# The last layer's attention scores in three rounded products, with the keys kept once

## The chip, the cores and the metric

The kernel runs on one core of a Trainium2 chip. The metric is the device time of one execution in microseconds; the span given with a profile is the time from its first to its last instruction.

## What is computed

A block of two attention layers over 512 tokens of width 1024 is followed by one hybrid layer. Its first half is an attention with three branches: over compressed keys, over chosen blocks of keys, and over a window. With 512 tokens, eight blocks of 64 and the best eight chosen, and with a window of 512, the last two branches each come to plain causal attention, with keys and values of their own. There are eight query heads of 64 elements; four of them share a key head (g).

```python
s_cmp = jnp.einsum('bgrsd,bgcd->bgrsc', qh, k_cmp) * SCALE
p_cmp = masked_softmax(s_cmp, cmp_end[None, :] <= pos[:, None])
...
_, sel_idx = lax.top_k(imp, top_n)

q_rot = partial_rope(qh, pos)
ks_blk = partial_rope(kvh(ks), pos).reshape(B, NSA_KV, n_sel, SEL_BLOCK, HEAD_DIM)
...
s_win = jnp.einsum('bgrqd,bgkd->bgrqk', qc, kwc) * SCALE
p_win = masked_softmax(s_win, w_mask)
o_win = jnp.einsum('bgrqk,bgkd->bgrqd', p_win, vwc.astype(f32))
...
o = g[..., 0:1] * o_cmp + g[..., 1:2] * unblock(o_sel) + g[..., 2:3] * unblock(o_win)
```

## The kernel before

**Rounded parts.** All large products of the kernel are made of three: each f32 operand is split into a high part (a copy in the rounded type, F32R) and a low part (the f32 value minus the high part, rounded too), and high x high, high x low and low x high are added in one PSUM bank. `second` holds, for some stretches of an SBUF tensor, a twin of type F32R at the same addresses; `rounded(v)` gives the twin of a view, `read_back(v)` reads it as f32. For the weights ScalarE writes the high part (`high`, line 1310) and GpSimd the low part in four quarters (`lower`, line 2506). The small products of the attention, the scores of the last layer among them, are plain f32 products.

**Banks and order.** Each engine has a list of its own instructions in the order of the program. TensorE takes the eight PSUM banks in turn: `begin(key, consumer)` makes TensorE wait until the bank of the key eight before is evacuated, and notes whether ScalarE ("a") or VectorE ("v") empties it; `end` tells that it is filled. `take` on the consumer waits for the filled bank, `give` tells that it is drained, `evacuated` waits for that. All matmuls have line 468 (`mm`), ScalarE's copies line 1281 (`copy`), semaphore waits of their own line 316 or 303.

**Before the steps.** Queries and keys of the last layer lie with tokens on partitions: q2 (for the compressed branch), q2r (rotated), kd (rotated keys of both branches b, each head twice side by side). After the product "hid" TensorE transposes them, for each of the four token tiles i: keys ("qp", i) (line 818), ("qr", i) (818) and ("kz", i) (822). ScalarE empties these banks (after a wait for three memsets of GpSimd, C_clear): qp into qTp and qr into qTr, both scaled by 1/8, and kz in two copies, partitions 0 to 63 into kz[..., e = 0, ...] and 64 to 127 into kz[..., e = 1, ...]; the other halves hold the zeros of a memset of 4096 columns on GpSimd (line 2617). Ahead of i = 2 ScalarE rounds the weights Cog0 (`high(HI[("Cog", 0)])`), behind the last tile Cog1. TensorE goes on with `gate_c(0)`, 24 products with Cog0, for whose quarters it waits on GpSimd, with kcmp and vcmp, `gate_c(1)`, the compressed scores `scores_c`, `gate_c(2)` and so on. VectorE makes hid_t (2148), then waits for the gate (2122), kcmp and vcmp.

**The steps.** The attention of the two branches runs in NSTEP = 12 steps s; each has four units u = 4s + m, one bank each. `cell(s, m)` gives head pair j = s // 3, query tile i, branches and e = m % 2 (head 2j + e, whose 64 elements lie on partitions 64e to 64e + 63). With k = s % 3: for k = 0 the units are query tiles 0, 0, 1, 1 with both branches in a bank (256 and 512 columns), for k = 1 query tile 2 (384 columns) for each branch and e, for k = 2 tile 3 (512 columns). TensorE's order is scoresN(s), transN(s-1), pvN(s-2): the scores and then the four causal masks (bf16, line 468, from identb and causalb), the transposes of the probabilities (line 904), and the products with the values. So the keys of a step are four ("NS", u), four ("NT", u), one ("NO", s). VectorE takes the maxima (2221) of step s, then, when ScalarE's exponentials are done, the reciprocals (2228) and the scaling of the probabilities (2236), ahead of it the output of step s-3 (`outN`, 2208, into mixA). ScalarE's order is the four units' exponentials of step s (1634), then the four copies of transposes of step s-1 (1281); in step 7 and step 9 it rounds weights for the next stage behind them.

**Areas.** The arena is one SBUF tensor. fl (the input of "hid") and mixA both lie at 15552 to 17600; kz takes 8192 to 12288.

Of the kernel before, what the change touches and what calls it, by code (L numbers as in the profile page):

```python
# [106 lines left out]
def program(nc, A, out):  # L107
    ctx = ExitStack()
    with ctx:
# [29 lines left out]
        arena = sb2("arena", [P, NARENA], (0, 12288), (19456, 6144))  # L139
# [230 lines left out]
        kz = area(8192, 4096).rearrange("p (b g e t) -> p b g e t", b=2, g=2, e=2)  # L370
# [74 lines left out]
        def _(pe):  # L445
# [368 lines left out]
            for i in range(NT):  # L814
                for name, src in (("qp", q2), ("qr", q2r)):
                    b = begin((name, i), "a")
                    for j in range(4):
                        ins = nc.tensor.transpose(b[:, j * P:(j + 1) * P], src[:, i, j * P:(j + 1) * P], ident)
                    end(ins)
                b = begin(("kz", i), "a")  # L820
# [45 lines left out]
            gate_c(1)  # L866
            evacuated(pe, ("kz", NT - 1))
# [12 lines left out]

            def scoresN(s):

                bs = []
                for m in range(4):
                    j, i, brs, e = cell(s, m)
                    n, nb, es = (i + 1) * P, len(brs), slice(64 * e, 64 * e + 64)
                    b = begin(("NS", 4 * s + m), "a")
                    k = ap(kz[es, brs[0], j // 2, e, :], [(2048, nb), (1, n)])
                    mm(b[:, 0:nb * n].rearrange("p (b n) -> p b n", b=nb), qTr[es, j, i * P:(i + 1) * P], k, True, False)
                    bs.append(b)  # L890
# [378 lines left out]
        def _(act):  # L1269
# [309 lines left out]
            act.wait_ge(S("C_clear"), 3)  # L1579
            for i in range(NT):  # L1580
                if i == 2:
                    high(HI[("Cog", 0)])
                for name, dst in (("qp", qTp), ("qr", qTr)):
                    key = (name, i)
                    b = take(act, key)
                    give(copy(dst[:, :, i * P:(i + 1) * P], b[:, :].rearrange("p (j t) -> p j t", j=4), 0.125), key)
                key = ("kz", i)
                b = take(act, key)
                for e in range(2):
                    es = slice(64 * e, 64 * e + 64)  # L1590
                    ins = copy(ap(kz[es, 0, 0, e, :], [(1024, 4), (1, P)], i * P), b[es, :].rearrange("p (j t) -> p j t", j=4))
                give(ins, key)
# [157 lines left out]
        def _(dve):  # L1750
# [397 lines left out]
            give(STT(hid_t, thh, 1.0, b[:, 0:256], ALU.add, ALU.mult), "hid")  # L2148
# [546 lines left out]
```

## Time and profile before

| | us |
|---|---|
| median of 3 runs | 1234.92 |
| lowest and highest | 1231.48, 1236.01 |
| profiled execution, its own time | 1235.75 |
| its span | 1234.0 |
| TensorE matmul busy | 1146.0 (93%) |
| TensorE weight load busy | 963.2 (78%) |
| VectorE busy | 592.1 (48%) |
| ScalarE busy | 509.0 (41%) |
| GpSimd busy | 452.0 (37%) |
| mean granted TensorE clock, share of full | 0.979 |

PE is the TensorE matmul, PEld its weight load, which overlaps it, DVE is VectorE, ACT ScalarE, POOL GpSimd, SP the queue of the loads. A row of the time line gives a start, a duration, the engine, line and operation, what is written and read, the rows and columns of the array (64*128), partitions and columns of the operand, the count of instructions merged, and in brackets the idle time before and what ended it. A matmul's duration holds its way through the array, so the pace of a stream is read from the starts of its instructions. An f32 type in these rows may be a rounded operand; such operands have "parts" in their names.

### The profile page before, as it was taken

The page shows a single profiled execution, that of the slowest core. Times are in us where ns is not written, and L with a number is a line of the kernel's source. Part 1 is how long each engine was busy: PE and PEld are TensorE (multiplying, and loading weights), DVE is VectorE, ACT ScalarE, POOL GpSimd, SP SyncE. Part 2 cuts the span into 40 slices and gives each one's busy share as a digit, 9 for nine tenths or more (in the row PEclk, how much of TensorE's full clock was granted, in tenths as well). Part 3 has the DMA queues.
Part 4 walks back from the last instruction along what each step waited for, and adds up shares of the span by engine and source line. Part 5 has one row for each costly group of instructions (what it writes and reads, how often), then busy time and mean ns, then how long its engine had stood idle before and what let it go on. Part 6 is the DMA issues. An engine that isn't in the chain of part 4 may idle for free.

```text
span 1234.0 us, 24860 instructions
## 1 busy us (share of the span) xinstructions
PE 1146.0 (93%) x10339; PEld 963.2 (78%) x10339; DVE 592.1 (48%) x1376; ACT 509.0 (41%) x1038; POOL 452.0 (37%) x391
## 2 busy tenths in 40 slices
PE   3999999999898999899998959988999999999995
PEld 3988887889898998656798958966777787778862
DVE  5000003842728158788417275026872577335546
ACT  4232224852424432688523264242883421233321
POOL 5744484884445445301344326320006452000000
PEclk9999999999999999999999989999999899999998
DMA  7433243323121232100231231262002223100001
GB/s 211 142 104 102 76 129 106 83 55 103 43 95 40 98 103 89 49 1 1 70 103 35 80 126 52 69 188 69 2 2 69 69 72 111 55 24 3 4 2 68
DMA packets 73178, 89.60 MB, mean 73 GB/s; under 512 B 1993, under 2 KB 66634, under 8 KB 72938
## 3 DMA queue, kind: packets, MB, share of 16 engines
q1 hardware_dynamic: 70136, 78.65, 20.0%
q0 software_dynamic: 2416, 8.26, 2.7%
q8 instruction: 82, 1.34, 0.5%
q10 hardware_dynamic: 514, 1.11, 0.4%
q14 instruction: 30, 0.25, 0.1%
HBM read 83.75 MB, written 4.26 MB: 71 GB/s over the span
## 4 chain that ended last, share of the span: by engine, by line
PE 79%; DVE 9%; ACT 5%; POOL 3%; issue 3%; DMA 1%; ACTq 1%; DVEq 0%; POOLq 0%
PE bank L468 73%; PE bank L736 2%; POOL ring_parts L2506 2%; ACT arena L1281 1%; PE bank L646 1%; DVE stat L1782 1%; PE bank L904 1%; DVE arena L1805 1%; ACT ring_parts L1310 1%; DVE stat L1783 1%; DVE x L1802 1%; ACT arena L1634 1%; ACT arena L1397 1%; DMA vrow<-in_cmp_pos_v 1%; DVE arena L1793 1%
## 5 line engine op out<-in xcount | busy, mean ns | idle before, releaser
L2506 POOL TENSOR_TENSOR ring_parts<-ring,ring_parts 128x512 fp32r<-128x512 f32 (+1 forms) x236 | 306.8, 1333 | 372.7 <-ACT ring_parts L1310 284.1
L468 PE MATMUL bank<-ring_parts,hT_parts 128*128 128x256 f32 x1664 | 331.0, 285 | 12.6 <-POOL arena_parts L2512 7.8
L468 PE MATMUL bank<-hT_parts,ring_parts 128*128 128x512 f32 x896 | 285.3, 397 | 8.7 <-DVE x L1802 4.8
L468 PEld LDWEIGHTS bank<-ring_parts,hT_parts 128*128 128x128 f32 x1664 | 269.8, 192 | 15.3 <-issue 11.2
L1281 ACT ACTIVATE arena<-bank 128x512 f32<-128x512 f32 (+3 forms) x356 | 166.7, 528 | 261.7 <-PE bank L468 253.7
L468 PE MATMUL bank<-ring_parts,arena_parts 128*128 128x256 f32 x1088 | 257.7, 285 | 3.4 <-POOL hT_parts L2523 3.4
L468 PE MATMUL bank<-arena 64*64 64x64 f32 (+6 forms) x3440 | 217.2, 275 | 7.6 <-ACT arena L1634 2.9
L468 PEld LDWEIGHTS bank<-hT_parts,ring_parts 128*128 128x128 f32 x896 | 171.0, 191 | 49.5 <-issue 6.6
L468 PEld LDWEIGHTS bank<-arena 64*64 64x64 f32 (+2 forms) x3440 | 157.1, 141 | 61.3 <-issue 23.5
L468 PEld LDWEIGHTS bank<-ring_parts,arena_parts 128*128 128x128 f32 x1088 | 190.8, 192 | 4.3 <-POOL hT_parts L2523 3.8
L1310 ACT ACTIVATE ring_parts<-ring 128x2048 fp32r<-128x2048 f32 (+1 forms) x59 | 111.3, 1886 | 76.9 <-PE bank L468 76.9
L468 PE MATMUL bank<-arena_parts,ring_parts 128*128 128x512 f32 x256 | 101.2, 395 | 0.0
L1857 DVE SCALAR_TENSOR_TENSOR arena<-arena,bank 128x512 f32<-128x512 f32 x8 | 5.5, 687 | 172.0 <-ACT arena L1385 172.0
L468 PE MATMUL bank<-x_parts,ring_parts 128*128 128x512 f32 x192 | 77.2, 402 | 0.0
L468 PEld LDWEIGHTS bank<-arena_parts,ring_parts 128*128 128x128 f32 x256 | 48.0, 188 | 10.7
L2523 POOL TENSOR_TENSOR hT_parts<-hT,arena_parts 128x512 fp32r<-128x512 f32 x16 | 20.4, 1280 | 92.1 <-ACT arena_parts L1336 91.9
L2512 POOL TENSOR_TENSOR arena_parts<-arena,hT_parts 128x512 fp32r<-128x512 f32 x26 | 34.4, 1350 | 44.2 <-ACT hT_parts L1315 44.2
L468 PE MATMUL bank<-ring,arena 64*64 64x64 f32 (+3 forms) x512 | 49.2, 304 | 0.8 <-DMA ring<-in_cmp_w_v 0.8
L1511 ACT ACTIVATE arena<-bank,stat 128x512 f32<-128x512 f32 x64 | 43.2, 688 | 14.1 <-PE bank L468 6.7
L1924 DVE TENSOR_TENSOR x<-x,bank 128x256 f32<-128x256 f32 x32 | 13.4, 420 | 70.9 <-PE bank L468 70.9
L2043 DVE TENSOR_REDUCE stat<-bank 128x1 f32<-128x512 f32 x64 | 39.8, 684 | 14.3 <-PE bank L468 14.3
L1946 DVE SCALAR_TENSOR_TENSOR arena<-arena,bank 128x256 f32<-128x256 f32 x32 | 13.4, 419 | 64.2 <-PE bank L468 58.5
(240 smaller groups left out, 1440.5 us busy)
## 6 DMA issues: line engine op xcount, KB each, us to landing
ring<-in_a_w_in SPq DMA_DIRECT2D x16, 1024.0 KB, 5.4
ring<-in_w_in SPq DMA_DIRECT2D x15, 1024.0 KB, 5.5
ring<-in_b_w_in SPq DMA_DIRECT2D x10, 1024.0 KB, 5.3
ring<-in_ple_w_gate SPq DMA_DIRECT2D x8, 1024.0 KB, 5.1
arena<-rpb_rows POOLq DMA_DIRECT2D x16, 256.0 KB, 3.5
ring<-in_a_w_out SPq DMA_DIRECT2D x4, 1024.0 KB, 5.1
ring<-in_b_w_out SPq DMA_DIRECT2D x4, 1024.0 KB, 5.3
ring<-in_w_out SPq DMA_DIRECT2D x4, 1024.0 KB, 5.0
```

Of the source, the lines that this page charges most:

```text
L468: return nc.tensor.matmul(o, l, r, start=start, stop=stop)
L646: ins = nc.tensor.transpose(b[:, o:o + P], pA[:, u % 8, o:o + P], ident)
L736: ins = nc.tensor.transpose(b[:, k * P:(k + 1) * P], pB[u % 8][:, k * P:(k + 1) * P], ident)
L1281: return nc.scalar.activation(o, i, ACT.Copy, scale=scale)
L1310: nc.scalar.activation(rounded(high_slot(n)[:, 0:m]), raw_slot(n)[:, 0:m], ACT.Copy).then_inc(s_whi, 1)
L1511: give(nc.scalar.activation(pB[u % 8], b[:, :], ACT.Exp, bias=stat[:, c:c + 1], accum_out=stat[:, c + 8:c + 9]), key)
L1924: give(TT(xs, xs, b[:, 0:w], ALU.add), key)
L1946: give(STT(tp[:, u % 2, :], thp[:, u % 4, :], 1.0, b[:, 0:256], ALU.add, ALU.mult), key)
L2043: nc.vector.tensor_reduce(stat[:, 128 + u % 8:129 + u % 8], b[:, :], X, ALU.max, negate=True)\
L2506: nc.gpsimd.tensor_tensor(rounded(r), r, read_back(high_slot(n)[:, o:o + m // 4]), ALU.subtract)\
L2512: nc.gpsimd.tensor_tensor(rounded(v), v, read_back(tile_of(hTf, tag, i, hf)), ALU.subtract)\
L2523: nc.gpsimd.tensor_tensor(rounded(hT[:, j, :]), hT[:, j, :], read_back(o_high[:, T * j:T * j + T]), ALU.subtract)\
```

## The change

Queries qTr and keys kz of the scores get a high part, written by ScalarE in the rounded type, and a low part, written by VectorE from the same bank and the high part; the low part of the queries lies in mixA, that of the keys in kz_lo, the second half of the old kz. The banks of qr and kz are thus emptied by VectorE, after ScalarE has read them (a new semaphore C_high). The keys lose the axis e: both heads' halves are written by one copy of 128 partitions, the memset is gone, and so is ScalarE's wait for C_clear; VectorE waits for two of these instead of three. TensorE also waits for the last qp. The scores of a unit become three products of 64 rows in place of one plain f32 product; all four banks of a step are taken first, then, for units 0 and 1 and again for 2 and 3, each of the three products is issued for both units in turn. The masks follow as before.

```diff
--- before.py
+++ after.py
@@ -136,7 +136,7 @@
         w2 = sb("w2", [P, 2, 2, HD])
         wa = sb("wa", [P, 512])
         NARENA = 27968
-        arena = sb2("arena", [P, NARENA], (0, 12288), (19456, 6144))
+        arena = sb2("arena", [P, NARENA], (0, 12288), (15552, 2048), (19456, 6144))
         bank = [ctx.enter_context(nc.psum_tensor(f"bank{b}", [P, 512], F32)) for b in range(NBANK)]
         x_kept = nc.dram_tensor("x_kept", [NT, P, D], F32, kind="Internal").ap()
         scratch = nc.dram_tensor("rpb_rows", [16, 1024], F32, kind="Internal").ap()
@@ -367,7 +367,8 @@
         q2r = area(2048, 2048).rearrange("p (i n) -> p i n", i=NT)
         qTp = area(4096, 2048).rearrange("p (j t) -> p j t", j=4)
         qTr = area(6144, 2048).rearrange("p (j t) -> p j t", j=4)
-        kz = area(8192, 4096).rearrange("p (b g e t) -> p b g e t", b=2, g=2, e=2)
+        kz = area(8192, 2048).rearrange("p (b g t) -> p b g t", b=2, g=2)
+        kz_lo = area(10240, 2048).rearrange("p (b g t) -> p b g t", b=2, g=2)
         vS = area(12288, 1024).rearrange("p (i b n) -> p i b n", i=NT, b=2)
         gt = area(14432, 96).rearrange("p (i n) -> p i n", i=NT)
         pTc = area(14528, 1024).rearrange("p (g t) -> p g t", g=2)
@@ -812,12 +813,12 @@
             used3(("W1V", 1))
             pe.wait_ge(S("C_rope"), 4)
             for i in range(NT):
-                for name, src in (("qp", q2), ("qr", q2r)):
-                    b = begin((name, i), "a")
+                for name, src, consumer in (("qp", q2, "a"), ("qr", q2r, "v")):
+                    b = begin((name, i), consumer)
                     for j in range(4):
                         ins = nc.tensor.transpose(b[:, j * P:(j + 1) * P], src[:, i, j * P:(j + 1) * P], ident)
                     end(ins)
-                b = begin(("kz", i), "a")
+                b = begin(("kz", i), "v")
                 for m in range(4):
                     ins = nc.tensor.transpose(b[:, m * P:(m + 1) * P], kd[:, i, m // 2, (m % 2) * P:(m % 2) * P + P], ident)
                 end(ins)
@@ -864,6 +865,7 @@
                              w2[:, 1, blk, :], blk == 0, blk == 1)
             end(ins)
             gate_c(1)
+            evacuated(pe, ("qp", NT - 1))
             evacuated(pe, ("kz", NT - 1))
             pe.wait_ge(S("C_cmp"), 12)
             scores_c(0)
@@ -878,16 +880,20 @@
             trans_c(3)
 
 
+            qn_parts = [rounded(v[:, :, :]) for v in (qTr, mixA)]
+            kn_parts = [rounded(v[:, :, :, :]) for v in (kz, kz_lo)]
+
             def scoresN(s):
 
-                bs = []
-                for m in range(4):
-                    j, i, brs, e = cell(s, m)
-                    n, nb, es = (i + 1) * P, len(brs), slice(64 * e, 64 * e + 64)
-                    b = begin(("NS", 4 * s + m), "a")
-                    k = ap(kz[es, brs[0], j // 2, e, :], [(2048, nb), (1, n)])
-                    mm(b[:, 0:nb * n].rearrange("p (b n) -> p b n", b=nb), qTr[es, j, i * P:(i + 1) * P], k, True, False)
-                    bs.append(b)
+                bs = [begin(("NS", 4 * s + m), "a") for m in range(4)]
+                for m0 in (0, 2):
+                    for a, c in ((0, 0), (0, 1), (1, 0)):
+                        for m in (m0, m0 + 1):
+                            j, i, brs, e = cell(s, m)
+                            n, nb, es = (i + 1) * P, len(brs), slice(64 * e, 64 * e + 64)
+                            k = ap(kn_parts[c][es, brs[0], j // 2, :], [(1024, nb), (1, n)])
+                            mm(bs[m][:, 0:nb * n].rearrange("p (b n) -> p b n", b=nb),
+                               qn_parts[a][es, j, i * P:(i + 1) * P], k, (a, c) == (0, 0), False)
                 for m, b in enumerate(bs):
                     j, i, brs, e = cell(s, m)
                     nb = len(brs)
@@ -1576,20 +1582,19 @@
             give(copy(gt[:, :, :], b[:, 0:96].rearrange("p (i n) -> p i n", i=NT)), "bgT")
             b = take(act, "hid")
             nc.scalar.activation(thh, b[:, 0:256], ACT.Tanh, scale=0.5).then_inc(S("C_thh"), 1)
-            act.wait_ge(S("C_clear"), 3)
             for i in range(NT):
+                ts = slice(i * P, (i + 1) * P)
                 if i == 2:
                     high(HI[("Cog", 0)])
-                for name, dst in (("qp", qTp), ("qr", qTr)):
-                    key = (name, i)
-                    b = take(act, key)
-                    give(copy(dst[:, :, i * P:(i + 1) * P], b[:, :].rearrange("p (j t) -> p j t", j=4), 0.125), key)
-                key = ("kz", i)
+                key = ("qp", i)
                 b = take(act, key)
-                for e in range(2):
-                    es = slice(64 * e, 64 * e + 64)
-                    ins = copy(ap(kz[es, 0, 0, e, :], [(1024, 4), (1, P)], i * P), b[es, :].rearrange("p (j t) -> p j t", j=4))
-                give(ins, key)
+                give(copy(qTp[:, :, ts], b[:, :].rearrange("p (j t) -> p j t", j=4), 0.125), key)
+                b = take(act, ("qr", i))
+                nc.scalar.activation(rounded(qTr[:, :, ts]), b[:, :].rearrange("p (j t) -> p j t", j=4), ACT.Copy, scale=0.125)\
+                    .then_inc(S("C_high"), 1)
+                b = take(act, ("kz", i))
+                nc.scalar.activation(rounded(kz.rearrange("p b g t -> p (b g) t")[:, :, ts]),
+                                     b[:, :].rearrange("p (j t) -> p j t", j=4), ACT.Copy).then_inc(S("C_high"), 1)
             b = take(act, "hidT")
             for n in range(2):
                 ins = copy(ap(hid[:, n, :], [(64, 2), (1, 64)]), ap(b[:, :], [(P, 2), (1, 64)], 64 * n))
@@ -2146,8 +2151,18 @@
             b = take(dve, "hid")
             dve.wait_ge(S("C_thh"), 1)
             give(STT(hid_t, thh, 1.0, b[:, 0:256], ALU.add, ALU.mult), "hid")
+            for i in range(NT):
+                ts = slice(i * P, (i + 1) * P)
+                for m, (name, low_part, high_part, scale) in enumerate((
+                        ("qr", mixA[:, :, ts], qTr[:, :, ts], 0.125),
+                        ("kz", kz_lo.rearrange("p b g t -> p (b g) t")[:, :, ts],
+                         kz.rearrange("p b g t -> p (b g) t")[:, :, ts], 1.0))):
+                    dve.wait_ge(S("C_high"), 2 * i + m + 1)
+                    b = take(dve, (name, i))
+                    give(STT(rounded(low_part), b[:, :].rearrange("p (j t) -> p j t", j=4), scale, read_back(high_part),
+                             ALU.mult, ALU.subtract), (name, i))
             gatesC([("og", 0)], "C_tanh", Gn)
-            dve.wait_ge(S("C_clear"), 3)
+            dve.wait_ge(S("C_clear"), 2)
 
             b = take(dve, "kcmp")
             for e in range(2):
@@ -2614,7 +2629,6 @@
             nc.gpsimd.memset(kcz[:, :, :, :], 0.0).then_inc(S("C_clear"), 1)
             nc.gpsimd.memset(vcz[:, :, :, :], 0.0).then_inc(S("C_clear"), 1)
             lower(HI[("Cq", 0)])
-            nc.gpsimd.memset(kz[:, :, :, :, :], 0.0).then_inc(S("C_clear"), 1)
             lower(HI[("Cq", 1)], HI[("Cog", 1)])
             pool.wait_ge(S("N_probs"), 4 * NSTEP)
             lower(HI[("R", 6)], HI[("R", 2)])
```

## Rows read from the trace of the kernel before

**Rows 1.** the page's chain that ended last, shares of the span by engine
```profile
PE 79%; DVE 9%; ACT 5%; POOL 3%; issue 3%; DMA 1%; ACTq 1%; DVEq 0%; POOLq 0%
```

**Rows 2.** the chain in order of time before the steps: start us, us, what
```profile
821.48 1.92 ACT ring_parts L1310
823.47 1.27 POOL ring_parts L2506
```

**Rows 3.** TensorE's time line, steps 3 to 6: start us, us, engine, line
```profile
870.69 0.73 PEld L468 LDWEIGHTS bank<-arena 64*128 64x128 f32 x8 [0.17 <-ACT arena L1634]
...
872.18 0.61 PE L468 MATMUL bank<-causalb,identb 128*128 128x256 bf16 x4
...
876.15 1.02 PEld L468 LDWEIGHTS bank<-arena 64*128 64x128 f32 x8 [0.17 <-issue]
...
877.72 0.40 PE L468 MATMUL bank<-causalb,identb 128*128 128x128 bf16 x4
...
881.64 0.30 PEld L468 LDWEIGHTS bank<-arena 64*128 64x128 f32 x4 [0.17 <-ACT arena L1281]
...
883.56 0.40 PE L468 MATMUL bank<-causalb,identb 128*128 128x128 bf16 x4
...
887.42 0.30 PEld L468 LDWEIGHTS bank<-arena 64*128 64x128 f32 x4 [0.17 <-ACT arena L1634]
```

**Rows 4.** groups of instructions in 881.5 to 883.9: busy us, mean ns of one
```profile
L468 PE MATMUL bank<-arena 64*128 64x512 f32 x8 | 2.0, 615 | 0.0
```

**Rows 5.** the time line, weights' products of 256 and 512 columns on TensorE
```profile
795.01 0.40 PE L468 MATMUL bank<-ring_parts,hT_parts 128*128 128x256 f32 x2
...
795.37 0.40 PE L468 MATMUL bank<-ring_parts,hT_parts 128*128 128x256 f32 x2
...
805.05 0.62 PE L468 MATMUL bank<-hT_parts,ring_parts 128*128 128x512 f32 x2
...
805.73 0.62 PE L468 MATMUL bank<-hT_parts,ring_parts 128*128 128x512 f32 x2
```

**Rows 6.** the time line, narrow windows: first copies of transposes, a load
```profile
870.54 0.50 ACT L1281 ACTIVATE arena<-bank 128x384 f32<-128x384 f32 x1
...
876.19 0.63 ACT L1281 ACTIVATE arena<-bank 128x512 f32<-128x512 f32 x1
...
876.88 0.21 PEld L468 LDWEIGHTS bank<-arena 64*128 64x128 f32 x2
...
880.95 0.39 ACT L1281 ACTIVATE arena<-bank 128x256 f32<-128x256 f32 x1
```

**Rows 7.** the time line of step 2: last score's load, masks' matmuls
```profile
865.77 0.29 PEld L468 LDWEIGHTS bank<-arena 64*128 64x128 f32 x2 [0.27 <-ACT arena L1634]
...
866.83 0.40 PE L468 MATMUL bank<-causalb,identb 128*128 128x128 bf16 x4
```

**Rows 8.** TensorE in the time line of step 10, at pvN(8)
```profile
914.26 4.10 PE L468 MATMUL bank<-arena 128*64 128x128 f32 x44 [1.29 <-ACT arena L1634]
```

**Rows 9.** the time line before the steps, on ScalarE, TensorE and VectorE
```profile
817.12 4.34 ACT L1281 ACTIVATE arena<-bank 128x512 f32<-128x512 f32 x8 [0.26 <-PE bank L818]
...
824.88 0.47 PE L468 MATMUL bank<-hT_parts,ring_parts 128*128 128x512 f32 x1 [2.84 <-POOL ring_parts L2506]
...
831.35 0.69 DVE L2122 SCALAR_TENSOR_TENSOR arena<-arena,bank 128x512 f32<-128x512 f32 x1 [13.94 <-ACT arena L1549]
```

**Rows 10.** the time line near 180 us: GpSimd's low parts beside VectorE reading PSUM
```profile
178.95 3.79 POOL L2506 TENSOR_TENSOR ring_parts<-ring,ring_parts 128x512 fp32r<-128x512 f32 x3
...
180.51 0.69 DVE L1857 SCALAR_TENSOR_TENSOR arena<-arena,bank 128x512 f32<-128x512 f32 x1 [4.87 <-ACT arena L1385]
```

**Rows 11.** the time line of GpSimd: the memset of kz and what follows
```profile
764.02 3.51 POOL L2617 MEMSET arena<- 128x4096 f32 x1
769.93 1.30 POOL L2506 TENSOR_TENSOR ring_parts<-ring,ring_parts 128x512 fp32r<-128x512 f32 x1 [2.40 <-ACT ring_parts L1310]
```

**Rows 12.** 845 to 851: busy us (PE, PEld, DVE, ACT, POOL), clock, DMA, GB/s
```profile
845.00:851.00 6.00, 5.25 (x26) 4.58 (x27) 4.44 (x12) 1.19 (x4) 0.00 (x0) 0.74 0.01 3
```

## Prediction

> **What bounds the kernel now.** I read the page's chain first: 79% of it is TensorE [rows 1]. Then I read the same chain in order of time around the last layer's attention, to see which pieces there are not TensorE [rows 2]. Before the attention steps the queue of TensorE stands still for 2.84 us until GpSimd has the first low parts of Cog0 [rows 9]; the chain goes ScalarE rounding (1.92 us), GpSimd (1.27 us), then TensorE [rows 2]. The steps themselves (scoresN, transN, pvN, twelve of them, in groups of three: k = 0, 1, 2) I read in the time line. From the first weight load of the scores of one group (870.69) to that of the next (887.42) is 16.73 us, in which the queue is nearly always busy. The three steps take 5.46, 5.49 and 5.78 us [rows 3]. So TensorE bounds this stage, and a shorter score phase would count in full, if nothing else of TensorE's turn got later.
>
> **The score phases now.** From the first load of the scores to that of the mask they take 1.49, 1.57 and 1.92 us for k = 0, 1, 2 [rows 3]. The last holds four scores of 512 columns in eight records of 615 ns each, but the union is 2.0 us [rows 4]: the scores of e = 0 and e = 1 (partitions 0 to 63 and 64 to 127) run side by side. Two pairs in 1.92 us, less some 0.2 us for the first load and for the change to the mask, is 0.86 us a pair, that is 0.43 us for each of the two records of a plain f32 matmul.
>
> **Three products instead.** No row shows a rounded product of 64 rows. The nearest are the weights' products of 128 rows: three of 512 columns start 0.68 us after the last three (805.05 to 805.73), so 0.227 each; three of 256 columns take 0.36 us, so 0.12 each [rows 5]. In between, 384 columns make 0.173. If a pair costs what one of these costs, the phases become, with the same 0.2 us: 3 x (0.12 + 0.227) + 0.2 = 1.24; 6 x 0.173 + 0.2 = 1.24; 6 x 0.227 + 0.2 = 1.56. That saves 0.25, 0.33 and 0.36 us, 0.94 a group, 3.8 us over four groups. The lower bound of a product is half of a plain record, 0.213 (and 0.107 for 256 columns), as the pairs now have it: then the savings are 0.33, 0.41 and 0.44. The upper bound is that pairs are lost (a rival below). I take the middle one, as it is a measured stream of the same kind of product.
>
> **The four banks taken at once.** This is the step I think decides. Now each score waits for its own bank just before its matmul. After, `begin` runs four times ahead of the first product, so the first product waits also for the fourth bank. In an order of nine keys a step over eight banks, the fourth bank of scoresN(s+1) is that of the first transposes of transN(s-1), and ScalarE copies these only after all exponentials of step s. The waiting TensorE has the whole of scoresN, transN and pvN queued behind it. When are those copies over now? At 870.54 + 0.50 = 871.04, at 876.19 + 0.63 = 876.82, at 880.95 + 0.39 = 881.34, and one group after the first at 871.04 + 16.73 = 887.77; and a load starts 0.06 us later (876.88) [rows 6]. Scores began at 870.69, 876.15 and 887.42 [rows 3]. So in two steps of three the fourth bank comes after the scores have begun. The copies move with the scores of their step, since exponentials wait for maxima and these for the mask. So:
> - k = 0 to 1: 876.88 - 870.69 - 0.25 = 5.94 us, against 5.46: 0.48 longer.
> - k = 1 to 2: here the copy is over at 881.34, before TensorE arrives at 881.64, so TensorE's own work binds: 5.49 - 0.33 = 5.16, 0.33 shorter.
> - k = 2 to 0: 887.83 - 881.64 - 0.36 = 5.83, against 5.78: 0.05 longer.
>
> A group comes to +0.20 us (with the lower bound of a product: +0.40 - 0.41 - 0.03 = -0.04). At the start the steps don't fit this. The scores of step 2 are now issued one by one as ScalarE frees the banks; the last load starts at 865.77 and the mask's matmul at 866.83 [rows 7]. After, all four start at 865.77 - 0.25 = 865.52 and the mask at 867.08, 0.25 later, and the scores of step 3 after the copy: 871.04 + 0.06 + 0.25 = 871.35 against 870.69, +0.66. Steps 3 to 8 add 2 x 0.20. In step 9 ScalarE also rounds weights, and TensorE waits 1.29 us for its next exponentials [rows 8]; that chain follows the scores of step 9, so it stands at +1.06 - 0.25 = +0.81, and the last score phase takes off 0.36. The stage ends +0.45 us later; with the lower bound of a product about -0.3. The 3.8 us are not lost to work, they turn into this wait.
>
> **Copies before the steps.** ScalarE now makes four copies a token tile (qp, qr, two halves of kz): eight in 4.34 us, 0.54 each, then it rounds Cog0 [rows 2, 9]. After, there are three a tile, so the rounding starts two copies earlier: -1.08 us. Its cover is none: TensorE waits 2.84 us for it [rows 9]. What is late next is GpSimd's 1.27 us, which moves along; the later chain over tanh, VectorE and TensorE starts from the same matmuls. VectorE gets eight subtractions of 128x512 out of PSUM, 0.69 us each as the nearest row [rows 10], 5.5 us in all. They follow ScalarE's copies one behind, lie in an idle stretch of VectorE and are over near 826, before anything on that engine is due (its next work starts at 831.35 after 13.94 us of idleness [rows 9]); the banks they free (qr, kz) are wanted one tile or more later. Queued behind them stand the gate product, kcmp and vcmp. Without that cover, each would cost 0.69. Would they slow GpSimd, which then makes the low parts that TensorE waits for? Such an instruction at 180.51 left GpSimd's three tiles at 3.79 us, 1.26 each [rows 10]: no. A rounded output may cost ScalarE nothing or as much as 0.1 us each; the four of them before Cog0's rounding would be 0.4 us.
>
> **At nothing:** the memset of kz leaves GpSimd (3.51 us), but after it GpSimd waited 2.40 us for ScalarE anyway [rows 11]; if that cover were gone it would still be a gain only. No transfer is added or moved; the wait for the clears on ScalarE had long been met; the new waits for qp's last tile and for C_clear 2 as well.
>
> **The sum.** -1.08 + 0.45 = -0.6 us; by the bounds -1.4 to -0.2. The profiled run took 1235.75 us (span 1234.0 us), 0.8 above the median of 1234.92. The runs of before differ by 4.5 us, so I put the sum on the median: 1234.3 us. Half a per cent (6.2 us) is about what a measurement of this kernel can tell from no change.
>
> **Rivals.**
> - The wait for the fourth bank costs nothing (the copies come in time once all is shifted). For it: one step of three has that slack. Against: the two rows above. Then 3.8 + 1.08 come off: 1230.0 us. Chance 0.14.
> - Slower: rounded products of 64 rows don't run side by side. For it: no row has such a product. Against: plain f32 ones do [rows 4]. Each pair then costs double: 1.04 + 1.04 + 1.36 = 3.44 us a group, 13.8 in all, inside the loop of waits: 1248.1 us. It passes the half per cent once half of the pairing is lost. Chance 0.08.
> - Weight loads show in each product (0.1 us, six a step, twelve steps): +7.2, 1241.5 us. Chance 0.04. This is what the page's rule gives.
> - The clock: the granted share was 0.74 in 845 to 851 [rows 12], between its levels of 2.4 and 1.2 GHz; a mean of 0.74 over 6 us is 3.1 us of them at 1.2 GHz, which cost 1.6 us. TensorE has less to do in the steps and waits more, so one such stretch may appear there: 1235.9. Or this one may go: 1232.7. Together 0.10; they lie within the range.
> - The edit doesn't do what it says (rounded copies or products that cost as plain ones): each product of 512 as a plain pair's 0.86 us would show at once as score phases of over 5 us. Chance 0.01.
>
> My forecast has 0.63. The range reaches to the first rival and, upwards, over a lost clock stretch and the scatter of the runs, up to where a quarter of the pairing is lost: 1229.5 to 1239.5 us. Faster by over 0.5% (under 1228.7): 0.06, the first rival with a clock stretch gone. Slower: the three rivals outside the range, 0.08 + 0.04 + 0.01 = 0.13. Within: the rest, 0.81.
>
> **What would show it.** Score phases of 1.24, 1.24 and 1.56 us (steps k = 0, 1, 2) with 12 records each in pairs; the first load of the scores 0.06 us behind ScalarE's first copy in two steps of three, the engine idle 0.3 to 0.6 us before it; the group at 16.9 us; the wait for Cog0's low parts at 1.8 us instead of 2.84. The prediction is wrong if the group falls to 15.8 us (first rival), or if the score phases exceed 2 us (second, third).

## The result and the profile after

| | before | after |
|---|---|---|
| median of 20 runs of each, us | 1235.79 | 1237.96 |
| lowest to highest | 1231.26 to 1237.73 | 1235.06 to 1240.62 |
| profiled execution: its own time | 1235.75 | 1235.06 |
| its span | 1234.0 | 1232.4 |
| mean granted TensorE clock | 0.979 | 0.977 |

The ratio is 1.0018, with a 95% interval of 1.001 to 1.0026: the changed kernel is 2.2 us longer, inside the half per cent, but more than nothing. The sum of the prediction said -0.6. The profiled execution of after is by chance a short one, so the two spans don't show the difference; the stages do. Single executions of 3919.8 us (the kernel before) and 4918.5 us (e11 below) are of the slow kind and are left out of every ratio.

The chain of after covers only part of its span, so I read it for nothing, and read the time line by stages. Its row of shares, beside [rows 1]:

```profile
PE 22%; DVE 1%; issue 1%; ACT 1%; POOL 1%; DVEq 0%; ACTq 0%; POOLq 0%
```

TensorE's time line of steps 3 to 6 in after, beside [rows 3]. Columns as there; in brackets is the idle time before the row and what ended it.

```profile
867.00 0.50 PE L469 MATMUL bank<-arena_parts 64*128 64x256 f32 x4 [0.42 <-ACT arena L1287]
...
868.25 0.61 PE L469 MATMUL bank<-causalb,identb 128*128 128x256 bf16 x4
...
873.04 0.62 PE L469 MATMUL bank<-arena_parts 64*128 64x384 f32 x4 [0.75 <-ACT arena L1287]
...
874.29 0.40 PE L469 MATMUL bank<-causalb,identb 128*128 128x128 bf16 x4
...
878.13 0.72 PE L469 MATMUL bank<-arena_parts 64*128 64x512 f32 x4
...
879.72 0.40 PE L469 MATMUL bank<-causalb,identb 128*128 128x128 bf16 x4
...
884.07 0.50 PE L469 MATMUL bank<-arena_parts 64*128 64x256 f32 x4 [0.42 <-ACT arena L1287]
```

Two things are to be seen. The score phases last 1.25, 1.25 and 1.59 us (first product to mask). And in two steps of three the engine stands idle, 0.42 and 0.75 us, until ScalarE's copy (L1287 here) frees the fourth bank. The group lasts 17.07 us, against 16.73.

The four products' records of step 5 in after, grouped over 877.9 to 880, beside [rows 4] (busy us, mean ns of one):

```profile
L469 PE MATMUL bank<-arena_parts 64*128 64x512 f32 x8 | 1.3, 414 | 0.0
...
L469 PE MATMUL bank<-arena_parts,arena_parts 64*128 64x512 f32 x4 | 0.8, 393 | 0.0
```

Twelve records of some 400 ns pass in 1.59 us: they run side by side, at the pace of [rows 5].

The time line before the steps in after, ScalarE and then TensorE, beside [rows 9]:

```profile
812.84 0.60 ACT L1287 ACTIVATE arena<-bank 128x512 f32<-128x512 f32 x1 [0.20 <-PE bank L819]
813.33 0.59 ACT L1593 ACTIVATE arena_parts<-bank 128x512 fp32r<-128x512 f32 x1
...
815.71 1.97 ACT L1316 ACTIVATE ring_parts<-ring 128x2048 fp32r<-128x2048 f32 x1
```

```profile
819.17 0.47 PE L469 MATMUL bank<-hT_parts,ring_parts 128*128 128x512 f32 x1 [1.35 <-POOL ring_parts L2521]
```

Six copies pass in 2.87 us (812.84 to 815.71), where eight took 4.36 (817.12 to 821.48, [rows 2, 9]); TensorE waits 1.35 us for Cog0's low parts in place of 2.84.

The time line of VectorE there; the second row answers to the last of [rows 9]:

```profile
820.16 1.29 DVE L2162 SCALAR_TENSOR_TENSOR arena_parts<-bank,arena_parts 128x512 fp32r<-128x512 f32 x2 [0.18 <-ACT arena_parts L1593]
825.60 0.69 DVE L2127 SCALAR_TENSOR_TENSOR arena<-arena,bank 128x512 f32<-128x512 f32 x1 [4.14 <-ACT arena L1555]
```

The eight subtractions are over at 821.45, and VectorE is idle for 4.14 us after them.

For all kernels I then read five stages from the starts of rows. A: first transpose of q to first product of Cog0. B: first score of step 0 to that of step 3. G: step 3 to 6 (6 to 9 is the same within 0.04). C: first score of step 9 to the first product behind the steps. D: from there to the end of the span, in which no line was changed.

| kernel | A | B | G | C | D |
|---|---|---|---|---|---|
| before | 8.52 | 15.26 | 16.73 | 23.60 | 306.2 |
| after | 7.03 | 17.32 | 17.07 | 23.03 | 308.2 |
| e1 after, again | 7.03 | 17.53 | 17.08 | 23.04 | 309.4 |
| e2 after, banks in twos | 7.03 | 15.76 | 16.32 | 23.19 | 309.5 |
| e3 before, four banks first | 8.52 | 18.53 | 17.90 | 23.62 | 306.0 |
| e4 before, keys once | 7.01 | 16.48 | 16.74 | 23.62 | 306.2 |
| e5 before, shifted by 120 | 8.52 | 16.55 | 16.73 | 23.60 | 308.9 |
| e6 after, shifted to 256 | 7.03 | 17.65 | 17.07 | 23.03 | 306.8 |
| e7 as e2, shifted to 256 | 7.03 | 15.70 | 16.31 | 23.17 | 306.7 |
| e8 after, kept busy | 7.03 | 16.31 | 17.06 | 23.03 | 306.8 |
| e9 before, again | 8.51 | 15.37 | 16.74 | 23.62 | 304.4 |
| e10 before, shifted by 256 | 8.52 | 15.37 | 16.74 | 23.62 | 305.0 |
| e11 all three | 7.03 | 16.26 | 16.32 | 23.18 | 306.3 |

A, G and C repeat within 0.03 us among kernels that have the same part. B depends on where TensorE's clock falls, D on that and on breaks of TensorE's work that are taken up below. Between A and the first score TensorE does the same in all kernels: it takes 29.8 us, and 30.5 to 31.4 in before, after, e3 and e5, where a stretch of 3.4 us at a granted clock of 0.5 falls into it. Ahead of A its work differs only by the idle instructions of the experiments, yet the start of A lies anywhere from 812.1 to 816.6 us; so a span of one execution says little, and times are compared by medians.

### The profile page after: what moved, and what is told of

Its sections match the earlier page's. It is cut to its first block and busy times, and to the rows that moved or that the text cites. A ratio compares the mean times of both kernels' runs of the same rounds, so it can differ in the third digit from the quotient of the medians.

```text
span 1232.4 us, 24990 instructions
## 1 busy us (share of the span) xinstructions
PE 1142.3 (93%) x10387; PEld 964.7 (78%) x10387; DVE 597.6 (48%) x1384; ACT 506.2 (41%) x1034; POOL 449.2 (36%) x390
## 3 DMA queue, kind: packets, MB, share of 16 engines
q8 instruction: 82, 1.34, 0.5%
q10 hardware_dynamic: 514, 1.11, 0.4%
## 5 line engine op out<-in xcount | busy, mean ns | idle before, releaser
L1287 ACT ACTIVATE arena<-bank 128x512 f32<-128x512 f32 (+2 forms) x344 | 160.9, 528 | 262.2 <-PE bank L469 253.3
L469 PE MATMUL bank<-arena 64*64 64x64 f32 (+7 forms) x3344 | 196.4, 267 | 7.0 <-ACT arena L1287 2.3
L469 PEld LDWEIGHTS bank<-arena 64*64 64x64 f32 (+3 forms) x3344 | 147.8, 140 | 55.5 <-issue 21.6
```

The lines of the kernel that those rows point to most:

```text
L469: return nc.tensor.matmul(o, l, r, start=start, stop=stop)
L1287: return nc.scalar.activation(o, i, ACT.Copy, scale=scale)
```

## The experiments

### The first four: the change's parts

The kernel after once more.

> The changed kernel once more, for a second profile and the scatter of its time. Theory A (TensorE waits for four banks at once, and the longer wait in step 2 lets its clock fall there): 2.2 us over the kernel before (1.2 to 3.2), a group of three steps in 17.1 us, and again a stretch of half clock between steps 0 and 2. Theory B (the steps are not the cause; stretches of half clock fall anywhere and happened to be more): the half-clock stretch of the first steps is not there again, and the time is within 1 us of the kernel before.

Measured: 1237.53 us, ratio 1.0012 (1.0002 to 1.0022). B is 17.53 and D is 309.4. The part after the steps is longer than before's in a second execution too; I had not costed anything there.

The kernel after, with the banks begun for two scores at a time:

```diff
-                bs = [begin(("NS", 4 * s + m), "a") for m in range(4)]
+                bs = []
                 for m0 in (0, 2):
+                    bs += [begin(("NS", 4 * s + m), "a") for m in (m0, m0 + 1)]
```

> As changed, but the banks are taken two at a time, just before the products of their pair. Theory A: the first pair no longer waits for ScalarE's first copy of transposes; group of three steps 15.8 to 16.0 us instead of 17.07, step 2's first pair starts about 0.6 us earlier than all four do now; the time 4 to 5 us below the kernel before (1.5 from the copies before the steps, 0.85 a group, the rest at the start). Theory B (the waits are not what costs): time and group as in the changed kernel, about 2 us over the kernel before.

Measured: 1233.88 us, ratio 0.9984 (0.9973 to 0.9995), 3.7 us below the kernel after as measured beside it (e1). The idle time ahead of the scores is gone. Its time line:

```profile
866.05 1.40 PE L469 MATMUL bank<-arena 128*64 128x128 f32 x22
867.38 0.51 PE L469 MATMUL bank<-arena_parts 64*128 64x256 f32 x4
```

G is 16.32, 0.75 below after's, and B 1.6 to 1.8 below. So the wait for four banks is what turned the shorter products into a longer stage. The second pair still waits a little: the phases of the three steps are 1.40, 1.55 and 1.59 us, so that G gains 0.41 against before and not the 0.94 of the shorter phases.

The kernel before, plain products, with only the four banks begun first:

```diff
+                bs = [begin(("NS", 4 * s + m), "a") for m in range(4)]
                 for m in range(4):
...
-                    b = begin(("NS", 4 * s + m), "a")
+                    b = bs[m]
```

> The kernel before (plain f32 scores) with only this changed: all four banks of a step are taken before its first score. Theory A: k = 0 to 1 takes 6.19 instead of 5.46 us, k = 2 to 0 6.19 instead of 5.78, the group 17.87 instead of 16.73; the time 3.5 us over the kernel before, 5 if the clock falls in the first steps. Theory B: no difference, since the copies come about when TensorE arrives.

Measured: 1238.64 us, ratio 1.0026 (1.0015 to 1.0038). The same gaps stand in its time line:

```profile
871.38 1.56 PE L468 MATMUL bank<-arena 64*128 64x256 f32 x8 [0.43 <-ACT arena L1280]
...
877.66 1.56 PE L468 MATMUL bank<-arena 64*128 64x384 f32 x8 [0.76 <-ACT arena L1280]
```

G is 17.90, 1.17 more than before's, and B is 3.3 us more (with the clock's fall in it, below). So these are the costs of the wait alone, without the change's gain. The two stages together would make 5.6 us, and the medians differ by 2.8; where the other 2.8 us are gained I can't say.

The kernel before, with the keys kept once (one copy of 128 partitions for two of 64; no memset of kz, no wait for it) and plain products:

```diff
-                for e in range(2):
-                    es = slice(64 * e, 64 * e + 64)
-                    ins = copy(ap(kz[es, 0, 0, e, :], [(1024, 4), (1, P)], i * P), b[es, :].rearrange("p (j t) -> p j t", j=4))
-                give(ins, key)
+                give(copy(kz.rearrange("p b g t -> p (b g) t")[:, :, i * P:(i + 1) * P],
+                          b[:, :].rearrange("p (j t) -> p j t", j=4)), key)
```

> The kernel before (plain f32 scores, banks one by one) with the keys kept once: one copy of 128 partitions in place of two of 64, no memset, no wait of ScalarE for the clears; no low parts. Theory A: TensorE waits 1.35 us instead of 2.84 for Cog0's low parts and the time falls by 1.5 us, the steps stay as they were (16.73 a group). Theory B: the gain of the copies doesn't reach the end (it is given back in the chain over tanh and VectorE): no difference, within 0.5 us.

Measured: 1232.5 us, ratio 0.9971 (0.9961 to 0.9981), 3.3 us below the kernel before. A is 7.01, so 1.5 us of it is seen; the rest I can't place (B is 1.1 us longer in its profile, all else as before). ScalarE's time line:

```profile
814.58 3.04 ACT L1281 ACTIVATE arena<-bank 128x512 f32<-128x512 f32 x6 [0.20 <-PE bank L818]
817.46 1.95 ACT L1310 ACTIVATE ring_parts<-ring 128x2048 fp32r<-128x2048 f32 x1
```

Six plain copies take 2.88 us, 0.48 each, and after's six with rounded outputs took 2.87: rounding costs ScalarE nothing. The four half-partition copies of before then took 4.36 - 4 x 0.48 = 2.44, 0.61 each. The records last 0.59 us or a little more in both kinds; behind a copy of 128 partitions the next starts 0.48 us after it, behind one of 64 partitions only when it is over. Why is not shown.

### Where the part behind the steps loses two to three microseconds

In after, a stretch of small products 155 us behind the steps is broken. First the kernel before, then after, the group of records of that line over 2.0 and 2.2 us:

```profile
L468 PE MATMUL bank<-ring,arena 64*64 64x64 f32 x64 | 1.2, 218 | 0.0
```

```profile
L469 PE MATMUL bank<-ring,arena 64*64 64x64 f32 x55 | 1.4, 219 | 0.8 <-issue 0.8
```

And in after's time line, then the DMA queues of 1078 to 1079:

```profile
1079.52 0.63 PE L469 MATMUL bank<-ring,arena 64*64 64x64 f32 x27
1080.97 0.45 PE L469 MATMUL bank<-ring,arena 64*64 64x64 f32 x7 [0.81 <-issue]
```

```profile
q8 instruction: 1, 0.02, 7.4%
```

To test it I moved the stream with products of one row and one column, four instructions each, ahead of norm2's transposes, where TensorE is idle for 10.7 us:

```diff
                 b = begin((tag, i, hf), "v")
+                if (tag, i, hf) == ("norm2", 0, 0):
+                    for _ in range(30):
+                        mm(b[0:1, 0:1], ident[:, 0:1], ident[:, 0:1], True, True)
+                    pe.wait_ge(S("xn_norm2"), 1)
```

> The kernel before with one edit that computes nothing new: 30 products of one row and one column are put into TensorE's stream ahead of the transposes that wait for norm2, where it stands idle for 10.7 us, and into a bank that these transposes overwrite. Each is 4 instructions, so all that follows stands 120 instructions later in the stream, as after the three-product change (48 more weight loads, 48 more matmuls, 24 more semaphore instructions). Theory that the 2 to 3 us lost after the steps are a fetch of TensorE's instructions that falls into a run of 64x64 products: the work from the first product after the steps to the end takes 308 to 309.5 us in place of 306.2, with a gap of about 1 us and the fetch beside it some 157 us after the steps, and the time is 2 to 3 us above before's. Rival, that the loss comes from the three products themselves (what they leave behind in queues, banks or the clock): 306.2 us there and no change of the time beyond 0.5 us.

Measured: 1237.94 us, ratio 1.0013 (0.9999 to 1.0027), 2.5 us above before's median. The interval just holds 1, so the time alone shows no loss; D is 308.9, against 306.2 and 304.4 in the two profiles of before (e9 is the second), and the same stretch breaks, with an instruction packet in 1084 to 1085 ahead of it:

```profile
L468 PE MATMUL bank<-ring,arena 64*64 64x64 f32 x58 | 1.4, 220 | 0.9 <-issue 0.9
```

```profile
q8 instruction: 1, 0.02, 6.6%
```

A kernel with none of the change has the change's loss behind the steps.

The kernel after with 34 of them (120 + 136 = 256):

> The kernel after with 34 such products of one row and one column in the same idle time: 136 more instructions, so that with the 120 of the change all that follows the steps stands 256 instructions, one fetch packet of 16 KB, later than in the kernel before. Fetch theory: the part after the steps is back to 306 to 306.5 us, and the time is 2 to 3 us below the kernel after's, about before's (1234.5 to 1236). Rival, that the three products leave something behind: 308 to 309.5 us there still, and 1237.5 to 1238.

Measured: 1234.72 us, ratio 0.9987 (0.9975 to 0.9999), which lies apart from both intervals of the unshifted kernel. D is 306.8 and the stretch is whole, though an instruction packet moves in 1083 to 1084 beside it; a packet alone breaks nothing:

```profile
L469 PE MATMUL bank<-ring,arena 64*64 64x64 f32 x64 | 1.2, 220 | 0.0
```

The kernel of the banks in twos with the same 34:

> The kernel after with the score banks asked for two at a time, as in the run that had it alone (1233.9, 2 us below before), and the 34 products of one column too. Fetch theory: the two gains add, as they lie in different stages: 2 to 3 us less than with the two banks alone, 1230.5 to 1232. Rival: no further gain, 1233.9.

Measured: 1232.53 us, ratio 0.9975 (0.9965 to 0.9986). D falls from 309.5 to 306.7. By the two medians the gain is 1.35 us, less than D's 2.8, and the intervals of the two ratios overlap: the time alone does not show it.

The kernel before with 64 of them, 256 instructions:

> The kernel before with 64 of the products of one row and one column in place of 30: 256 instructions, one fetch packet of 16 KB, so that every packet border falls on the same instruction as in the kernel before. Theory, that the place of the border decides: 306.2 to 306.5 us after the steps, and the time within 0.5 us of before's. Rival, that more instructions or the added products cost by themselves: at least the 2.5 us of the run with 30 of them, 308.5 us or more after the steps and 1238 or more.

Measured: 1234.66 us, ratio 0.9996 (0.9985 to 1.0007); D is 305.0. Twice the added work costs nothing where half of it cost 2.5 us. By the stages it is the position that decides, not the work added; the ratios of e5 and e10 alone, whose intervals overlap, would not show it. e3 fits too: it moves the stream by only 23 instructions in its trace, and D is 306.0.

The traces show more. The broken stretch is one of three places in after:

```profile
1119.67 0.33 PE L1119 MATMUL bank<-cst,hT 128*128 128x128 f32 x1 [1.11 <-ACT arena L1287]
...
1158.10 0.27 PE L1119 MATMUL bank<-cst,arena 128*128 128x128 f32 x1 [0.40 <-issue]
```

In before TensorE doesn't wait at all ahead of these three products. Together they are 2.3 us (0.81, 1.11, 0.40), and TensorE's idle time from the steps to its last product is 10.75 us in after against 8.40 in before. So what D loses is not one break but three. The three are there in e1, e2 and e5 as well (idle 10.3, 10.0 and 10.7 us), and in none of e3, e6, e7, e9 and e11 (8.4 to 8.6).

They all have one place in TensorE's stream. In after, e1, e2 and e5 alike, 15809 of TensorE's recorded instructions start ahead of the first of the three products, and 17601 and 19393 ahead of the other two: 7 x 256 and 14 x 256 more. Smaller or single breaks stand at the same places in e4 (0.24 us behind 15809), e10 (0.46 us behind 16065, which is 256 more) and e8 (1.27 us behind 19393). Each of these breaks ends 2.2 to 2.9 us after the start of an instruction packet. The load of final_g, which runs beside the first break, runs beside the same products in before and e6 without one, and at the second and third break of after no data moves but the instruction packet. So the breaks come once in a whole number of packets, and beside a packet's arrival. That the instruction behind a border waits for its packet is inferred from this; most borders pass without a break, and what decides it at each is not shown.

### The clock in the first steps

In after, TensorE is idle for much of 853 to 860 us, and its granted clock falls. The windows of two microseconds (busy us of PE, PEld, DVE, ACT, POOL, then the clock):

```profile
853.00:855.00 2.00, 0.85 (x6) 0.40 (x4) 1.49 (x6) 2.00 (x10) 0.00 (x0) 1.00 0.48 166
855.00:857.00 2.00, 1.00 (x6) 0.87 (x5) 1.84 (x6) 0.09 (x1) 0.00 (x0) 0.71 0.00 0
857.00:859.00 2.00, 1.10 (x6) 0.69 (x4) 1.96 (x6) 1.72 (x7) 0.00 (x0) 0.50 0.00 0
859.00:861.00 2.00, 1.22 (x6) 1.11 (x8) 1.65 (x5) 2.00 (x7) 0.00 (x0) 0.50 0.01 4
```

and the scores of step 2 fall into it, after a wait for all four banks:

```profile
859.78 1.22 PE L469 MATMUL bank<-arena_parts 64*128 64x512 f32 x4 [1.69 <-ACT arena L1639]
```

At 1.2 GHz (0.50) they take 2.86 us in place of 1.59. I kept the engine busy with products that nothing reads, two ahead of each first wait for probabilities, and four, two, two as step 2's banks come free:

```diff
-                bs = [begin(("NS", 4 * s + m), "a") for m in range(4)]
+                bs = []
+                for m in range(4):
+                    bs.append(begin(("NS", 4 * s + m), "a"))
+                    if s == 2 and m < 3:
+                        for _ in range((4, 2, 2)[m]):
+                            mm(bs[m][:, :], qn_parts[0][:, 0, 0:P], kn_parts[0][:, 0, 0, :], True, True)
```

> The kernel after with 16 more rounded products of 512 columns that nothing reads, 0.23 us each, put into the waits of steps 1 and 2: two ahead of each of the four waits for the first probabilities, and four, two and two into the score banks of step 2 as they come free. They keep TensorE busy where it stood idle for 3.8 of 7 us and its clock then fell to half for 6.8 us. If the lower clock is what the start of the steps lost beyond the forecast, the granted clock stays at 1 up to the steps' end, the scores of step 2 take about 1.3 us in place of 2.9, and the time from the first to the fourth step's scores is 15.5 to 16.3 us in place of 17.3 to 17.5, some 1 to 2 us off the whole. Rival, that step 2 waits for ScalarE and VectorE and the clock costs nothing: the same 17.3 us or more (up to 1 us more, where the added products stand in the way), and no gain in the whole.

Measured: 1233.29 us, ratio 0.9987 (0.9977 to 0.9996). The clock holds:

```profile
857.00:859.00 2.00, 1.55 (x10) 1.19 (x10) 2.00 (x6) 0.67 (x3) 0.00 (x0) 1.00 0.00 0
859.00:861.00 2.00, 1.95 (x8) 1.43 (x8) 1.88 (x7) 2.00 (x9) 0.00 (x0) 1.00 0.00 0
```

The scores of step 2 take 1.59 us and B is 16.31, 1.0 to 1.3 below the three profiles of the kernel after with four banks. D is 306.8 here too: with 32 more weight loads and products the stream moves again, and only one of the three breaks is left. So the clock's share is read from B and not from the time.

The kernel before, once more:

> The kernel before, unchanged, profiled once more. What it is for: whether the fall of TensorE's clock in the first steps belongs to the change or is before's too. If it is before's too in other executions (as in the kernel before with shifted instructions: 16.5 us from the first to the fourth scores, step 2's scores 4.1 us), then some 1.3 us of what the kernel after seemed to lose in the start of the steps is no loss, and the 15.3 us of the first profile was a lucky one. If the kernel before keeps 15.2 to 15.4 us with step 2's scores at 2.8 us, the fall is the change's. After the steps 306.2 us either way, and a ratio of 1.000 within 0.0012.

Measured: 1234.8 us, ratio 1.0002 (0.9991 to 1.0012). B is 15.37, and here the clock falls too:

```profile
861.00:863.00 2.00, 1.47 (x7) 1.47 (x8) 2.00 (x7) 0.32 (x1) 0.00 (x0) 0.63 0.00 0
863.00:865.00 2.00, 2.00 (x7) 1.38 (x6) 1.96 (x6) 2.00 (x8) 0.00 (x0) 0.52 0.01 4
```

It fell for 3.4 us here, while step 2's scores waited for ScalarE anyway, and cost 0.1. In e4 and e5 (before's steps) the 3.4 us came 2 to 3 us later and cost 1.2. So a fall belongs to the old steps as well, but in the profiles of after, e1, e3 and e6, all with four banks at once, it lasts 6.8 us, in those with before's order or banks in twos 3.4 or none.

All together: banks in twos, products to keep the engine busy (four ahead of each pair in step 2), and 26 of the small products:

> All that the runs so far point to, in one kernel: the kernel after with the score banks asked for two at a time, the 16 rounded products that keep TensorE busy in the waits of steps 1 and 2, and 26 products of one column, so that with the rest the shift is 256 instructions. If the three causes are independent, it stands 2.9 us (two banks and shift, measured against before) and about 1 us (clock) below before: 1231 to 1232, with 15 us or less from the first to the fourth scores, groups of 16.3 us and 306.2 to 306.8 us after the steps. If the kept clock gives nothing beside the two banks (the clock fell for 3.4 us only there), it is the same 1232.5.

Measured: 1230.21 us, ratio 0.996 (0.9947 to 0.9973), from four executions. It is the lowest median of all, though its interval overlaps with e7's, and it is not reached by the way expected: B is 16.26, more than e7's 15.70. The added products of the second pair stand in its way:

```profile
860.99 1.87 PE L469 MATMUL bank<-arena_parts 128*128 128x512 f32 x8
862.70 0.39 PE L469 MATMUL bank<-arena_parts,arena_parts 64*128 64x512 f32 x2
```

The first row holds four added products beside the four records of the pair; the phase is 2.94 us at full clock. Where the 2.3 us against e7 come from I can't say; in the profile, D gives 0.4 and the start of A lies 1.0 us earlier, in a part that is the same in both but for eight of the small products.

## Why the prediction was right or wrong, step by step

- **The score phases** were forecast at 1.24, 1.24, 1.56 and are 1.25, 1.25, 1.59 us. The 64-row products run in pairs at the pace of the 128-row ones of [rows 5]. The rival of lost pairing and that of visible weight loads are dead: in step 3 of after the 512-column products of one half of the rows start at 867.43, 867.66 and 867.89, 0.23 us apart, though each has a load with a record of 0.18 us. The Trainium skill, page "TensorE: Matmul & The Clock Gate", Part 3, "The mechanism", lists that a weight load overlaps running matmuls only when its row group is another one. These rows don't agree with that as it stands; the same section also lets a load go ahead into a background weight buffer, which no row here can tell from it.
- **The four banks** were the right mechanism. The periods were forecast at 5.94, 5.16, 5.83 and are 6.04, 5.09, 5.94 us; the group 16.93, measured 17.07. ScalarE's first copy came as forecast (over 5.90 and 5.79 us behind the first score, forecast 5.88 and 5.77); what was too small is the 0.06 us from its end to TensorE: the first product starts 0.15 us behind it. The wait costs 0.68 us over two groups, not 0.40. e2 and e3 show it from both sides. The first rival (1230.0) falls with them.
- **The start of the steps** is a failed step, by size: +0.66 forecast, and 17.32 - 15.26 = +2.1 measured (15.37 in e9, 17.53 in e1). e8 splits it: some +1.0 is left with the clock held (16.31 against 15.3), the other 1.0 is the clock. Up to 0.3 of what is left is the price of the added products: from step 1 to step 2 e8 takes 8.58 us and after 8.32. I had seen that TensorE waits more there and had priced a clock stretch at 1.6 us, but only as a rival with a chance; it came in all four profiles of kernels with the four-bank wait where nothing kept the engine busy.
- **Stage end:** from step 9 on I took off 0.61 (0.25 + 0.36); measured 23.60 - 23.03 = 0.57.
- **Copies before the steps:** forecast -1.08, measured -1.49. The failed step is the mean of 0.54 a copy: it mixed four plain copies of 0.48 with four of 64 partitions at 0.61, and the edit replaces two of these by one plain one, for each of two tiles: 4 x 0.61 - 2 x 0.48 = 1.48. Rounded outputs cost nothing (e4 against after), and VectorE's subtractions had their cover. This error made the forecast too small a gain and did not cause the wrong sign.
- **Behind the steps** is the other failed step: I had put this part at nothing, without a word on it, and 2 to 3 us went there in after, e1 and e2. What was missing in the sum is the place of TensorE's instructions in their stream: breaks of 0.81, 1.11 and 0.40 us, 2.3 us together, at places whole packets of instructions apart. With it undone (e6) the kernel after is 1234.72, 0.7 below before's 1235.46, where -0.6 was forecast. That agreement is no evidence for the rest of the sum: with the two other errors mended, the copies (-0.4) and the steps (+1.7), it would have said +0.7.

Measured stages add to -1.49 + 2.1 + 0.68 - 0.57 + D's 2.0 = +2.7, and the medians say +2.2. That they are so near is in part luck: the same sum of stages gives +5.4 for e3, where the medians say +2.8, and -1.6 for e11, where they say -5.1. The time lies inside the range given and no change of over half a per cent was right, but the sign of the sum was wrong, because of what was left out behind the steps and of the start of the steps with its clock.

What stays open: apart from the breaks, D differs with the clock. In before (306.2) and e9 (304.4), the same kernel with the same idle time, TensorE's half-clock stretch some 46 us behind the steps lasts 10.2 and 6.8 us. A further one of 3.4 us some 360 us behind the first scores stands in all kernels with the rounded products but e11, shifted or not, and in none with plain ones; no run tells what it costs, or why it is there. Nor does a run explain where the medians of e3, e4 and e11 part from their stages.

## What to carry to other kernels

Ask for a buffer just before its first use: taking four at once made the first product wait for the last bank and turned 0.94 us of shorter work a group into 0.34 us more. Where a wait of the bounding engine grows, price the clock's fall in the next work as part of the wait, and not as a chance. And where a change adds instructions to the bounding engine, test a difference of 0.2% against the old kernel with as many idle instructions put in, before it is ascribed to the change's own work; and read the time behind the change for breaks at products where the old kernel has none.

## What the runs showed of the hardware

- TensorE's instructions come in packets of 16 KB, 256 instructions each (21109 for 82 packets in before). At places whole packets apart the engine can stand still: 0.81, 1.11 and 0.40 us behind its instructions 15809, 17601 and 19393 in after, whose distances are multiples of 256. Each break ends 2.2 to 2.9 us after the start of a packet. 120 idle instructions bring the three about in the old kernel (e5, D 308.9 against 306.2 and 304.4); with 256 only one of 0.46 us is left (e10, D 305.0).
- Rounded products of 64 rows run in pairs: twelve of 512 columns in 1.59 us with the change to the mask, at 2.4 GHz, and in 2.86 us at 1.2 GHz.
- ScalarE copies 512 columns from PSUM in 0.48 us on 128 partitions, rounded or not, and in 0.61 on 64 partitions, where the next copy starts only when the first is over.
